# One decoder layer on one core: FFN up projection as seven half products, with its own down stage

## The reference

```python
x = x + jnp.sum(gates * proj, axis=2) @ lp['w_out']
u = rmsnorm(x, lp['norm_ffn']) @ lp['w_up']
u, ffn_new = causal_dwconv(ffn_hist, u, lp['conv_f_w'], lp['conv_f_b'])   # width 3
ua, ub = jnp.split(u, 2, axis=-1)
x = x + (jax.nn.gelu(ua) * ub) @ lp['w_down']
x = x + jax.nn.sigmoid(rmsnorm(x, lp['norm_ple']) @ lp['w_ple_gate']) * (pe.astype(dt) @ lp['w_ple'])
```

## Time and profile before

| | us |
|---|---|
| median of 3 runs | 1867.05 |
| the profiled execution | 1866.39 |
| its span, first to last instruction | 1864.7 |
| TensorE busy in the span | 1838.9 |
| VectorE, ScalarE, GpSimd busy | 1007.3, 578.3, 407.4 |
| out projection's last matmul to first up product | 968.7 to 970.6 |
| one double tile (two up pairs, one down round) | 69.6 |
| last gate matmul ends | 1858.1 |

### The profile page before, as it was taken

How to read it: one execution, slowest core, us unless ns; L and a number is a source line. 1 busy time by engine, 2 the same in 40 slices (tenths; PEclk the granted TensorE clock), 3 DMA queues, 4 the chain that set the end, 5 groups by cost and what they waited for, 6 DMA issues and landing times.

```text
span 1864.7 us, 28730 instructions
## 1 busy us (share of the span) xinstructions
PE 1838.9 (99%) x11905; PEld 1787.3 (96%) x11905; DVE 1007.3 (54%) x1186; ACT 578.3 (31%) x779; POOL 407.4 (22%) x205
## 2 busy tenths in 40 slices
PE   8999999999999999999999999999999999999999
PEld 8999899987789999999999999999999999999999
DVE  7942585616763212124326676676676676675622
ACT  5423533135661212112334131131131131133621
POOL 1332222221122212221222131132132132132131
PEclk9999999999999999999999999999999999999999
DMA  6212212253252122124212111011111111010221
GB/s 216 38 58 80 66 62 83 75 168 114 75 180 76 63 82 103 46 81 138 91 36 91 35 56 45 34 57 44 34 61 40 34 66 38 31 68 1 89 81 47
DMA packets 55256, 134.30 MB, mean 72 GB/s; under 512 B 12898, under 2 KB 29826, under 8 KB 52866
## 3 DMA queue, kind: packets, MB, share of 16 engines
q1 hardware_dynamic: 43218, 105.94, 16.7%
q0 software_dynamic: 5040, 18.47, 3.1%
q10 hardware_dynamic: 6912, 8.65, 1.3%
HBM read 110.82 MB, written 22.31 MB: 71 GB/s over the span
## 4 chain that ended last, share of the span: by engine, by line
PE 93%; DVE 3%; ACT 2%; issue 1%; DMA 1%; POOL 0%; SPq 0%; ACTq 0%; DVEq 0%; POOLq 0%
PE ps L720 61%; PE ps L705 10%; PE ps L1169 9%; PE pst L1169 3%; PE ps L892 2%; PE ps L805 1%; PE ps L977 1%; PE ps L747 1%; PE ps L1011 1%; PE pst L998 1%; PE ps L692 1%; DMA masks<-in_wb 1%; DVE BIG L2292 1%; PE ps L753 0%; DVE Ml L2221 0%
## 5 line engine op out<-in xcount | busy, mean ns | idle before, releaser
L2487 POOL TENSOR_TENSOR Ul<-BIG,Uh 128x1024 fp32r<-128x1024 f32 x59 | 143.9, 2438 | 721.7 <-ACT Uh L1683 666.1
L720 PE MATMUL ps<-Nh,Uh 128*128 128x352 f32 x1248 | 270.4, 325 | 0.3 <-DVE H L2397 0.3
L720 PE MATMUL ps<-Nh,Ul 128*128 128x352 f32 x1248 | 268.9, 323 | 0.0
L720 PE MATMUL ps<-Fl,Uh 128*128 128x352 f32 x1248 | 268.7, 323 | 0.0
L720 PEld LDWEIGHTS ps<-Nh,Ul 128*128 128x128 f32 x1248 | 214.3, 188 | 0.0
L720 PEld LDWEIGHTS ps<-Nh,Uh 128*128 128x128 f32 x1248 | 212.6, 189 | 1.2 <-issue 0.9
L720 PEld LDWEIGHTS ps<-Fl,Uh 128*128 128x128 f32 x1248 | 211.9, 188 | 0.0
L720 PE MATMUL ps<-Hh,Uh 128*128 128x352 f32 x912 | 198.2, 325 | 2.6 <-DVE Ml L2221 2.3
L720 PE MATMUL ps<-Hh,Ul 128*128 128x352 f32 x912 | 196.5, 323 | 0.0
L2251 DVE TENSOR_TENSOR BIG<-BIG,ps 128x1056 f32<-128x1056 f32 x32 | 40.1, 1254 | 231.4 <-PE ps L720 225.1
L720 PEld LDWEIGHTS ps<-Hh,Uh 128*128 128x128 f32 x912 | 154.9, 189 | 4.9 <-DVE Ml L2221 2.3
(11 more groups left out here) (357 smaller groups left out, 3152.1 us busy)
## 6 DMA issues: line engine op xcount, KB each, us to landing
BIG<-in_wu SPq DMA_DIRECT2D x44, 512.0 KB, 3.8
H<-in_wd SPq DMA_DIRECT2D x11, 1024.0 KB, 4.8
BIG<-in_wgl SPq DMA_DIRECT2D x20, 512.0 KB, 4.3
gates<-BIG ACTq DMA_DIRECT2D x48, 176.0 KB, 2.0
BIG<-in_wz POOLq DMA_DIRECT2D x16, 512.0 KB, 3.9
BIG<-in_x SPq DMA_DIRECT2D x15, 528.0 KB, 7.0
BIG<-gates SPq DMA_DIRECT2D x12, 528.0 KB, 3.7
BIG<-in_wge POOLq DMA_DIRECT2D x12, 512.0 KB, 3.8
```

Of the source, the lines that this page charges most:

```text
L720: ins = nc.tensor.matmul(psb(3 * out + g), w[wp][:, k], x[xp][k][:, t0:t0 + n], start=(k == 0 and wp == xp), stop=(k == kk - 1 and wp == 1))
L2487: nc.gpsimd.tensor_tensor(Ul[:, half], uraw[:, half], Uh[:, half].bitcast(F32), ALU.subtract)\
```

## The change

Features and tokens are cut in halves: activations A11, A12, A21, A22 (first index the token half of 528, second the feature half), and the weights of a tile pair B11, B21 (tile of `ua`), B12, B22 (tile of `ub`). Seven products of half the depth and half the tokens give what eight gave (Strassen's scheme in Winograd's form). The activations' sums S1 to S4 are made once; the weights' sums T1 to T4 are made for every pair by GpSimd, in float32, before the split.

- A product is 4 row blocks x 3 parts x 2 groups of 264 tokens = 24 matmuls. The seven run in the order B11, T2, T3, B21, T1, T4, B22 on four pairs of PSUM banks (`PAIR_OF`); B21 adds onto the banks of B11, B22 onto those of T1.
- ScalarE copies B11's result (`m1`) and, after B21 was added to it, the first half of Y[0]. VectorE forms the rest by five additions (`u_sum`).
- The norm's factor is multiplied into X before the products (`shaped`: five blocks on VectorE, three on GpSimd), X itself is kept in DRAM (`kept_x`) and fetched again after the last product.
- The gated activations go to DRAM tile by tile (`hidden`). The down projection runs as a stage of its own after all up products, 11 rounds of 24 pieces, and fetches them from there.
- The embedding products (8 x 18 matmuls) are made right after the out projection, from buffers of their own, copied by ScalarE and kept in DRAM (`embedded`), and are fetched in the last stage.
- Loops of these stages are written out; y is stored by SyncE.

The core of the diff, with twelve columns of indent taken off:

```diff
...
-FIRST_D, FIRST_N = 5, 16
-DOWN_BANKS = (3, 4, 5, 6, 7, 0, 1, 2)
+B11, T2, T3, B21, T1, T4, B22 = range(7)
+PAIR_OF = (3, 2, 1, 3, 0, 1, 0)
+ROUNDS = NF // 2
+DOWN_BANKS = (6, 7, 4, 5, 2, 3, 0, 1)
...
# SyncE
+def up_weights(c):
+    for half in range(2):
+        sp.dma_start(wraw[c % 2][:, half], a["wu"][c, :, half]).then_inc(S(UP_SEMS[c % 2]), 16)
...
+for c in range(NF):
+    if c + 2 < NF:
+        sp.wait_ge(S("w_lo"), WLO + 7 * (c + 1))
+        up_weights(c + 2)
+    if c == NF - 1:
+        sp.wait_ge(S("up_done"), 7 * (NF - 1) + T2 + 1)
+        down_in(0)
+    if c:
+        hidden_out(c - 1)
+sp.wait_ge(S("up_done"), 7 * NF)
+sp.wait_ge(S("u_out"), 5 * NF)
+for c in range(KD):
+    sp.dma_start(X[:, c], kept_x[c]).then_inc(S(f"x_in{c // 2}"), 16)
+    if c == 2:
+        down_in(1)
...
# TensorE
+pe.wait_ge(S("n2_h"), 1)
+pe.wait_ge(S("d_lo"), 1)
+for d in range(KD):
+    if d == 0:
+        pe.wait_ge(S("r_added"), KD)
+    elif d == 1:
+        pe.wait_ge(S("n1_ln"), 4)
+    else:
+        pe.wait_ge(S("p_sig"), d - 1)
+    dense3(1 - d % 2, (Ph[:, :, d], Pl[:, :, d]), (chunks(Eh), chunks(El)), KP, None,
+           (0, last_square) if d == 0 else None).then_inc(S("p_gate"), 1)
...
+def product(c, b):
+    pe.wait_ge(S("w_lo"), WLO + 7 * c + b + 1)
+    if b == B11:
+        if c:
+            pe.wait_ge(S("u_copied"), 2 * c)
+        else:
+            pe.wait_ge(S("shaped"), 9)
+    elif b == T2:
+        if c:
+            pe.wait_ge(S("u_out"), 5 * (c - 1) + 1)
...
+    elif b == T3:
+        if c:
+            pe.wait_ge(S("u_out"), 5 * (c - 1) + 4)
...
+    elif b == B21:
+        pe.wait_ge(S("u_copied"), 2 * c + 1)
...
+    elif b == T1:
+        if c:
+            pe.wait_ge(S("u_out"), 5 * c)
...
+    elif b == T4:
+        pe.wait_ge(S("u_out"), 5 * c + 2)
...
+    else:
+        pe.wait_ge(S("u_out"), 5 * c + 3)
...
+    xh, xl = OPERANDS[b]
+    fresh = b not in (B21, B22)
+    for k in range(KH):
+        for w, x in ((Wh, xh), (Wh, xl), (Wl, xh)):
+            for g in range(2):
+                ins = nc.tensor.matmul(pair(PAIR_OF[b])[:, g], w[:, b, k],
+                                       x[:, k, g * QUARTER:g * QUARTER + QUARTER],
+                                       start=(fresh and k == 0 and w is Wh and x is xh),
+                                       stop=(k == KH - 1 and w is Wl), skip_group_check=True)
+    ins.then_inc(S("up_done"), 1)
+for c in range(NF):
+    for part in range(7):
+        product(c, part)
...
-def up(i, q, half):
...
-    dense3(1 - half, (Uh[:, half], Ul[:, half]), normed_x, KD,
-           ("n2_h", 0) if first_block else None, (5, last_square) if first_block else None)\
-        .then_inc(S(f"u_done{half}"), 1)
...
# ScalarE
+def up_high(c, b):
+    if b in (B11, B21, B22):
+        act.wait_ge(S(UP_SEMS[c % 2]), 48 + 32 * (c // 2 + 1))
+    else:
+        act.wait_ge(S("up_raw"), 4 * c + {T1: 1, T2: 2, T4: 3, T3: 4}[b])
+    if c:
+        act.wait_ge(S("up_done"), 7 * (c - 1) + b + 1)
+    elif b == B11:
+        act.wait_ge(S("n2_h"), 1)
+        act.wait_ge(S("d_lo"), 1)
+    src = T1r if b == T1 else T4r if b == T4 else Wr[:, b] if b in (T2, T3) else block(c % 2, b)
+    nc.scalar.activation(Wh[:, b], src, ACT.Copy).then_inc(S("late_hi"), 1)
...
+def fresh_half(c, half):
+    src = Y[:, half]
+    act.wait_ge(S("u_out"), 5 * c + (4 if half == 0 else 5))
+    if half == 0:
+        act.wait_ge(S("u_copied"), 2 * c + 2)
...
+    if c:
+        if half == 0:
+            act.wait_ge(S("hidden_out"), 16 * c)
+        else:
+            act.wait_ge(S("g_made"), c)
+    nc.scalar.activation(V[:, half], src, ACT.Identity, scale=fpar[:, c, 4 * half + 2:4 * half + 3],
+                         bias=fpar[:, c, 4 * half + 3:4 * half + 4]).then_inc(S("u_tap"), 1)
+def gelu_half(c):
+    act.wait_ge(S("u_tapped"), 2 * c + 1)
+    nc.scalar.activation(V[:, 0], V[:, 0], ACT.Gelu_apprx_tanh).then_inc(S("u_gelu"), 1)
...
+for c in range(NF):
+    if c:
+        fresh_half(c - 1, 1)
+        gelu_half(c - 1)
+    act.wait_ge(S("up_done"), 7 * c + 1)
+    if c:
+        act.wait_ge(S("u_out"), 5 * c)
+    nc.scalar.activation(quarters(m1), pair(PAIR_OF[B11]), ACT.Copy).then_inc(S("u_copied"), 1)
+    if c == 0:
+        operand_high(A22h, A22)
+        act.wait_ge(S("shaped"), 10)
+        operand_high(S4h, S4r)
+        up_high(0, T4)
+    up_high(c, B22)
+    if c + 1 < NF:
+        for part in (B11, T2, T3):
+            up_high(c + 1, part)
+    else:
+        down_high(0)
+    act.wait_ge(S("up_done"), 7 * c + B21 + 1)
+    if c:
+        act.wait_ge(S("u_tapped"), 2 * c - 1)
+    else:
+        act.wait_ge(S("tile_out0"), 128)
+    nc.scalar.activation(quarters(Y[:, 0, 0:HALF]), pair(PAIR_OF[B21]), ACT.Copy).then_inc(S("u_copied"), 1)
+    if c + 1 < NF:
+        for part in (B21, T1, T4):
+            up_high(c + 1, part)
+    fresh_half(c, 0)
...
# VectorE
+dve.wait_ge(S("norm_rs"), 2)
+for c in range(5):
+    dve.wait_ge(S("mix_hi"), KD + c + 1)
+    v.tensor_tensor(X[:, c], X[:, c], nRS, ALU.mult).then_inc(S("shaped"), 1)
+dve.wait_ge(S("shaped"), KH)
+v.tensor_tensor(S3r, A11, A21, ALU.subtract).then_inc(S("shaped"), 1)
+dve.wait_ge(S("shaped"), 5)
+dve.wait_ge(S("shaped_p"), 3)
+v.tensor_tensor(S1r, A21, A22, ALU.add).then_inc(S("shaped"), 1)
+dve.wait_ge(S("shaped"), 7)
+v.tensor_tensor(S2r, S1r, A11, ALU.subtract).then_inc(S("shaped"), 1)
...
+def u_sum(dst, x, b):
+    v.tensor_tensor(quarters(dst), quarters(x), pair(PAIR_OF[b]), ALU.add).then_inc(S("u_out"), 1)
+def taps(c, half):
+    dve.wait_ge(S("u_tap"), 6 * c + 3 * half + 3)
+    y, x = V[:, half], Y[:, half]
+    w0, w1 = fpar[:, c, 4 * half:4 * half + 1], fpar[:, c, 4 * half + 1:4 * half + 2]
...
+    link(tap(w1, 1),
+         v.scalar_tensor_tensor(ys[:, :, 1:], xs[:, :, 0:3], w1, ys[:, :, 1:], ALU.mult, ALU.add),
+         v.scalar_tensor_tensor(ys[:, :, 0:1], fh[:, :, 1:2], w1, ys[:, :, 0:1], ALU.mult, ALU.add))
+    samples = (v.scalar_tensor_tensor(ys[:, :, 2:], xs[:, :, 0:2], w0, ys[:, :, 2:], ALU.mult, ALU.add),
+               v.scalar_tensor_tensor(ys[:, :, 0:2], fh, w0, ys[:, :, 0:2], ALU.mult, ALU.add))
+    link(*samples, tap(w0, 2))
+    dve.sem_inc(S("u_tapped"), 1)
+def hide(c):
+    dve.wait_ge(S("u_gelu"), c + 1)
+    v.tensor_tensor(V[:, 0], V[:, 0], V[:, 1], ALU.mult).then_inc(S("g_made"), 1)
...
+for c in range(NF):
+    if c:
+        taps(c - 1, 1)
+        hide(c - 1)
+    dve.wait_ge(S("up_done"), 7 * c + T2 + 1)
+    dve.wait_ge(S("u_copied"), 2 * c + 1)
+    u_sum(u2, m1, T2)
+    if c == 0:
+        operand_low(A22l, A22, A22h, 6)
+    dve.wait_ge(S("up_done"), 7 * c + T3 + 1)
+    dve.wait_ge(S("u_out"), 5 * c + 1)
+    u_sum(u3, u2, T3)
+    if c == 0:
+        operand_low(S4l, S4r, S4h, 7)
+    dve.wait_ge(S("up_done"), 7 * c + T1 + 1)
+    dve.wait_ge(S("u_out"), 5 * c + 2)
+    if c == 0:
+        for q in range(2):
+            dve.wait_ge(S(f"tile_out{q}"), 128)
+    u_sum(Y[:, 1, HALF:T], u3, T1)
+    if c == NF - 1:
+        hidden_low(0)
+    dve.wait_ge(S("up_done"), 7 * c + T4 + 1)
+    u_sum(Y[:, 0, HALF:T], u3, T4)
+    if c < NF - 1:
+        taps(c, 0)
+    dve.wait_ge(S("up_done"), 7 * c + B22 + 1)
+    u_sum(Y[:, 1, 0:HALF], u2, B22)
...
# GpSimd
+def up_sums(c):
+    e = c % 2
+    b11, b21, b12, b22 = wraw[e][:, 0, 0:KH], wraw[e][:, 0, KH:KD], wraw[e][:, 1, 0:KH], wraw[e][:, 1, KH:KD]
+    pool.wait_ge(S(UP_SEMS[e]), 48 + 32 * (c // 2 + 1))
+    if c:
+        pool.wait_ge(S("w_lo"), WLO + 7 * (c - 1) + T4 + 1)
...
+    nc.gpsimd.tensor_tensor(T1r, b12, b11, ALU.subtract).then_inc(S("up_raw"), 1)
+    pool.wait_ge(S("up_raw"), 4 * c + 1)
+    if c:
+        pool.wait_ge(S("up_done"), 7 * (c - 1) + T2 + 1)
+    nc.gpsimd.tensor_tensor(Wr[:, T2], b22, T1r, ALU.subtract).then_inc(S("up_raw"), 1)
+    pool.wait_ge(S("up_raw"), 4 * c + 2)
+    nc.gpsimd.tensor_tensor(T4r, b21, Wr[:, T2], ALU.subtract).then_inc(S("up_raw"), 1)
+def third_sum(c):
+    e = c % 2
+    pool.wait_ge(S("up_raw"), 4 * c + 3)
+    if c:
+        pool.wait_ge(S("up_done"), 7 * (c - 1) + T3 + 1)
+    nc.gpsimd.tensor_tensor(Wr[:, T3], wraw[e][:, 1, KH:KD], wraw[e][:, 1, 0:KH], ALU.subtract)\
+        .then_inc(S("up_raw"), 1)
+def up_low(c, b):
+    pool.wait_ge(S("late_hi"), WHI + 7 * c + b + 1)
+    if c == 0 and b == T4:
+        pool.wait_ge(S("r_ss"), KD - 1)
+    src = T1r if b == T1 else T4r if b == T4 else Wr[:, b] if b in (T2, T3) else block(c % 2, b)
+    nc.gpsimd.tensor_tensor(Wl[:, b], src, Wh[:, b].bitcast(F32), ALU.subtract).then_inc(S("w_lo"), 1)
+def up_split(c, bs):
+    for b in bs:
+        if b == T3:
+            third_sum(c)
+            pool.wait_ge(S("up_raw"), 4 * c + 4)
+        up_low(c, b)
+up_sums(0)
+up_split(0, range(T1 + 1))
+pool.wait_ge(S("norm_rs"), 2)
+for c in range(5, KD):
+    pool.wait_ge(S("mix_hi"), KD + c + 1)
+    nc.gpsimd.tensor_tensor(X[:, c], X[:, c], nRS, ALU.mult).then_inc(S("shaped_p"), 1)
+pool.wait_ge(S("n_hi"), 1 + 2)
```

(59 more changed lines are left out.)

746 lines of the change are left out of this document (335 added, 411 removed).

## The result

The changed kernel takes 1912.26 us (median, 1911.67 to 1913.23) where the kernel before took 1867.75 beside it: a ratio of 1.0239, 95% interval 1.0221 to 1.0256. The forecast was 1906. By stages, from the two profiled executions (spans 1909.9 and 1864.7 us).

| stage | predicted | measured |
|---|---|---|
| out projection ends 977.2 in place of 968.7 | 0 | +8.5 |
| head of the up stage 34.0 (was 3.6) | +31.1 | +30.4 |
| up stage 534.5 (was 512.6) | +25.4 | +21.9 |
| down stage 261.8 (was 254.0) | +5 | +7.8 |
| end | -22.2 | -23.3 |

A forecast was written before the change was run, and what follows sets the result against it. TensorE was taken to bound the kernel before. Up stage +25.4, head +31.1, down stage +5 and end -22.2 gave +39.3 us on 1866.4: forecast 1906 us, 8-in-10 range 1820 to 1950.

The forecast's parts named there:

- end: Last stage: embedding products leave the path (20.4 us) and the tail follows about 1.8 us sooner, together -22.2 us.
- The up stage's mechanism: Up stage: VectorE and GpSimd hold each other up in a 24.8 us loop; TensorE idles about 4 us; +25.4 us.
- The holds in the loop: Up-stage round: waits from the exclusion of 1.2, 1.2, 0.2 and 1.3 us; without them the loop is 20.9 us.
- the exclusion: A VectorE instruction with both operands in SBUF and a GpSimd subtraction cannot overlap; 22.6 us shared a pair.
- rival A: Up stage: TensorE sets the pace, the exclusion costs little; rounds of 20.9 us, total time 1819 us; chance 0.20.
- One reading behind it: Earlier trace: a VectorE sum with one PSUM operand took its usual 1.25 us wholly inside a 2.39 us GpSimd subtraction.
- Rival B: Up stage: a 264-column matmul gets no shorter, 0.1594 us; 26.8 us a pair, total time 1957 us; chance 0.06.
- Proportional surcharge: Up-stage matmul: the time above streaming shrinks with the columns, 119.5 to 121.4 ns; the same surcharge gives 122.7 to 125.1.
- Rival C: Up stage: shared work packs without waste; rounds 21.9 to 23.7 us, total time 1842 to 1881 us; chance 0.17.
- The head: Out projection's end to first up product: norm, scalings and sums take 34.7 us for 3.6, +31.1; embeddings cost nothing.
- The down stage: 252.5 us of matmuls as before, plus about 5 us for X's return and round 1's low parts behind a GeLU product.
- The break-even: Up stage: a round of about 23.0 us would leave the total time unchanged.

The follow-up runs named there:

- run 1: Changed kernel with no two-SBUF-operand VectorE operation in the up stage and the small taps left out (hidden wrong): 1833.74 us.
- run 2: Changed kernel with only the eight small taps of each tile pair left out, big taps and product of the halves kept: 1884.15 us.
- run 10: Changed kernel with 3 of the 18 matmuls cut from seven of the eight embedding products in the head: 1910.49 us.
- run 4: Changed kernel with the seven low parts of each tile pair's weights but the first made by VectorE, not GpSimd: 1915.84 us.

## Why the prediction was right

- The up stage's mechanism, its place and its size held: rounds of 24.1 for 24.8 us, the gaps where they were said to be, the small tap of 1.26 us beside GpSimd's 1.30 (unhindered 1.28 to 1.30, the line through the earlier trace rows gave 1.30). The holds in the loop were put at 3.9 us and are 3.3, which is most of the 0.7 us between 24.8 and 24.1. Runs 1 and 2 together show the exclusion as the cause of at least 2.3 us a round; without it the estimated loop is 20.8 us, which is rival A's 20.9.
- One reading behind it was not right: the sum of the earlier trace rows does not lie wholly inside the subtraction. It begins at 569.69 and ends at 570.94, and the subtraction ends at 570.57. It still began in the middle of one and took its usual time, and run 1 shows two such instructions side by side.
- The matmul of 264 columns costs 0.1220 us, priced 0.1236. Rival B (0.1594) was wrong. Proportional surcharge (0.1195 to 0.1214) and fixed one (0.1227 to 0.1251) bracket it.
- Rival C, lossless packing at 21.9 to 23.7, has its place in the chances still: 24.1 lay just outside it. No run tests it: where the rounds came down to 20.5 us, the shared work had been made less or taken apart.
- The head: 34.0 for 34.7 us, part by part: 7.2 us to the first scaling for 7.1, 12.8 for the scalings for 13.4, 13.9 to the first product for 14.0. The embeddings in it are free, as run 10 shows. Only with VectorE alone in it (27.7 us) do they come close.
- The down stage: +7.8 for +5. The round's second stall, 4.7 us, is the low part of round 1 behind the GeLU product, as said:

```profile
1548.99 11.54 DMA BIG<-kept_x
...
1564.52 1.92 ACT Dh L1924
1566.44 1.86 ACT Gh L1926
...
1568.36 4.86 issue
```

  VectorE's low part (line 2535) took 4.98 us here and not the 2.35 that the sum had, beside GpSimd's subtraction of 4.57: the same exclusion, which I had not counted there, and about the 2.8 us that the term was too small by.
- What failed: the out projection was put at nothing. The store of X, the scaling behind it and the 6.04 us subtraction were all in the diff; I followed them to their own results and not to what is queued behind them. +8.5 us, more than the whole error of 6. So the nearness of the total is in part luck: out projection and down stage came 11.3 us dearer than forecast, the other three stages 5.3 us cheaper.
- The break-even stood at a round of 23.0. With the stages as they came it is 24.1 - 45.3 / 22 = 22.0, so run 2's 22.8 was still slower than before. And the busy share of TensorE in the stage was 89%, not 84%: it is 87% in rounds at a clock of 1.00, since a record reaches past the next start, and 92% in rounds with a stretch at half clock.

## What to carry to other kernels

When an algorithm takes work off the busiest engine and gives it to two that share something, add up the shared time first: here 22.6 us shared against 20.8 on TensorE, in a loop of waits, turned the stage's gain of 56 us into a loss of 22, and seven subtractions moved to the faster of the two, with one store issued earlier, made it a gain of 52. After each such move ask what was late just behind: the store's wait in run 4 cost 77 us and did not show before. And when an experiment takes out several operations, a second one has to price those that only came along: the small taps were 1.3 of run 1's 3.6 us. Work for later belongs behind what the next tile needs, in every queue it passes.

## What was not expected of the hardware

TensorE's granted clock fell to its 1.2 GHz level after short waits. In the kernel before it was 1.00; in the changed kernel a stretch with a 2.3 us wait is followed, 2 us later, by 3 us at 0.50 (columns as in the earlier trace rows):

```profile
1165.00:1170.00 5.00, 3.17 (x26) 2.95 (x25) 3.31 (x5) 2.62 (x5) 0.00 (x0) 1.00 0.00 0
...
1172.00:1175.00 3.00, 3.00 (x16) 3.00 (x15) 2.80 (x3) 0.00 (x0) 3.00 (x2) 0.50 0.29 97
```

Such stretches recur round after round up to 1320 us and once more near 1365, and the rounds stay at 24.1 us, since TensorE catches up in its next wait. The same waits in the four rounds from 1062 us and the five from 1400 are followed by none (1.00 throughout), so what decides it stays open. After the 6.58 us stall of the out projection, where TensorE sets the pace, the clock was 0.50 for 4.7 us, and the 288 matmuls from its end on took 48.96 us for 46.61: 2.4 us more. A gap costs more than its length only where nothing absorbs it.
